# Feed-forward down passes: one tile operation a step, four split buffers for the last pass, and a last tile finished in halves

## The chip, the cores and the metric

One core of one Trainium2 chip runs the kernel as a single program. The metric is the device time of one execution in microseconds (us); the times given are medians of repeated executions. Five engines work side by side, each on its own instruction stream, and meet only at semaphores: TensorE (PE; its weight loads are listed as PEld), VectorE (DVE), ScalarE (ACT), GpSimd (POOL) and SyncE (SP), which here issues the transfers.

## The reference, cut to what matters

The program is one layer of a streaming encoder over 2048 prompt rows and 128 sample rows (8 streams of 16). The change lies in its last stage, the feed forward and the final norm, all in float32:

```
h2 = _rmsnorm(x, g_ffn) * (1 + sc2) + sh2
g = h2 @ f_w_gate
u = h2 @ f_w_up
gconv, new_fconv = _causal_dwconv(g, f_conv, f_conv_w, f_conv_b)
x = x + gt2 * ((jax.nn.silu(gconv) * u) @ f_w_down)
...
y_prompt = _rmsnorm(xp, g_final)
y_sample = _rmsnorm(xs, g_final)
```

The model width is 1024 and the inner width is 2816, which is 22 slices of 128.

## The kernel before

The 2176 rows are 17 tiles of 128 rows: tiles 0 to 15 are prompt, tile 16 is the sample. `feed_forward` takes them in three spans: span 0 has tiles 0 to 5, span 1 has tiles 6 to 11, span 2 (`LAST`) has tiles 12 to 16. For each span all gate and up products come first and leave `mid` (22 slices f, up to 768 columns) in SBUF. Then come two **down passes** a = 0 and a = 1, written (span, a) below: pass (0,0) has tiles 0 to 2, pass (0,1) tiles 3 to 5, and so on; pass (2,0) has tiles 12 to 14 and pass (2,1), the last, only tiles 15 and 16.

A down pass has 22 steps, one for each slice f. Every float32 operand is split into a high and a low part, and three products (high by high, high by low, low by high) are added up in PSUM. So a step needs, in this order: a 512 KB load of the slice of `f_w_down` into `raw[j]` (SP, j = f % 2); its high part `w_hi[j]` and that of `mid`, `m_hi[j]` (ACT); the low parts `w_lo[j]` and `m_lo[j]` (DVE); and 6 matmuls of 512 columns for each tile (PE), 18 a step, or 12 in the last pass. There are two buffers of each kind. ACT may write `w_hi[j]` for step f only when PE has finished step f - 2 (`s_used`), and SP may load `raw[j]` again only when `w_lo[j]` has been made from it (`s_lo`). In pass (2,1) the raw slices alternate between `raw` and two further places, `raw_far`, in columns of `mid` that span 2 does not use. The first and last steps of a pass are written out (`static_until`), the ones between are a hardware loop; pass (2,1) is written out whole.

The tiles of a finished pass are completed inside the first steps of the next pass, or of the next span's gate and up steps. A tile takes five **tile operations**: `gated` (DVE: PSUM sum times the gate, into `prod`), `residual` (DVE: add to the row tile `xr`), `squares` (ACT: sum of squares), two small operations on POOL that make `rstd`, and `finish` (DVE: times `rstd` and the final weight, into the one tile `y`). Then SP issues `store` (512 KB of `y`) and behind it the load of the `xr` of two tiles later. `tile_part(k, ...)` sets which of these follow step k. SP runs its list strictly in order, so a `store` that waits for `y` holds every load that stands behind it.

In passes (0,1), (1,1) and (2,1) the tile operations of the pass before stand like this: two `gated` after step 0, one `residual` after step 1, then `residual`, `gated` and `finish` after step 2, `residual` and `finish` after step 3, `finish` after step 4; the three stores stand in SP's list after the loads of steps 3, 4 and 5. After step 21 of pass (2,1) nothing is left to cover tiles 15 and 16: both are completed one after the other with the engines otherwise empty. In pass (2,1) PE also turns the convolution's kept rows with 22 small matmuls (`turn_tail`, L2987): 16 after step 5 and 6 after step 19.

Of the kernel before, what the change touches and what calls it, by code (L numbers as in the profile page):

```python
# [11 lines left out]
P = 128  # L12
# [2679 lines left out]
def feed_forward_tiles(nc, ctx):  # L2692
# [29 lines left out]
    for name in ("ss", "mean", "rstd"):  # L2722
        tile(name, [P, 2])
    flat = F["mid"][:].rearrange("p f t -> p (f t)")
# [30 lines left out]
def feed_forward(nc, sem, A, O, S, c, F, ffn_first, m_stored):  # L2755
# [4 lines left out]
    with ExitStack() as ctx:  # L2760
# [16 lines left out]
        raw_far = [mid[:, 4 + KD * j:4 + KD * (j + 1), last_width:last_width + P] for j in range(2)]  # L2777
        acc = ps("acc_ps", [P, 4, 2, 512])
# [8 lines left out]
        s_far = [sem(f"w_far_loaded{j}") for j in range(2)]  # L2787
        s_mhi, s_mlo = sem("mid_hi_done"), sem("mid_lo_done")
# [40 lines left out]
        def static_until(s, a):  # L2829

            if pieces(s, a):
                return 1, 1 + KD
            return 3, KF // 2 - 1

        def raw_of(f):

            return raw[f % 2][:].rearrange("p (k c) -> p k c", k=KD) if f % 4 < 2 else raw_far[f % 2]
# [4 lines left out]
        def _(sp):  # L2842
# [12 lines left out]
            def load_dn_last(f):  # L2855
                j, base = f % 2, down_unit(LAST, 1, 0)
                sp.wait_ge(s_lo[j], base + max(0, f // 2 - 1))
                if f % 4 < 2:
# [21 lines left out]
            for s in range(NSP):  # L2880
# [14 lines left out]
                for a in range(NPASS):  # L2895
                    if s == LAST and a == 1:
                        for f in range(KF):
                            load_dn_last(f)
                            if f >= 3 and f - 3 < len(before(s, a)):
                                store(before(s, a)[f - 3])  # L2900
                        continue
                    lo, hi = static_until(s, a)
                    for f in range(2 * lo):
                        load_dn(s, a, f // 2, f % 2)
                        if f >= 3 and f - 3 < len(before(s, a)):
                            store(before(s, a)[f - 3])
# [7 lines left out]
            for i in tiles_of(LAST, 1):  # L2914
                store(i)
            sp.wait_ge(s_tk, 6)
            sp.dma_start(O["s_ffn_conv"][0].rearrange("b j n -> (b j) n"), rows_out[0:16]).then_inc(s_tout, 16)
            sp.dma_start(O["p_ffn_conv"][0, 0], rows_out[16:18]).then_inc(s_tout, 16)
            sp.wait_ge(s_tout, 32)
            sp.wait_ge(s_store, 16 * (NT + 1))  # L2920

        @block.tensor
        def _(pe):
# [32 lines left out]
            def down_step(s, a, q, j):  # L2956
# [3 lines left out]
                for n, i in enumerate(tiles_of(s, a)):  # L2960
# [15 lines left out]
                    for lhs, rhs, begin in ((m_hi, w_hi, start), (m_hi, w_lo, False), (m_lo, w_hi, False)):  # L2976
                        for half in range(2):
                            last = t.matmul(acc[:, pair, half, :], lhs[j][:, cols], rhs[j][:, half * 512:(half + 1) * 512],  # L2978
                                            start=begin, stop=(stop and lhs is m_lo))
                last.then_inc(s_used[j], 1)  # L2980

# [15 lines left out]
            for s in range(NSP):  # L2997
# [5 lines left out]
                for a in range(NPASS):  # L3003
                    lo, hi = static_until(s, a)
                    for f in range(2 * lo):
                        down_step(s, a, f // 2, f % 2)
                    if s == LAST and a == 1:
                        for r in range(4):
                            turn_tail(r, (s_read, first_tile[s] + 3))
                        for f in range(2 * lo, 2 * hi):  # L3010
                            down_step(s, a, f // 2, f % 2)
                        for r in range(4, 6):
                            turn_tail(r, (s_tk, r - 3))
                        for f in range(2 * hi, KF):
                            down_step(s, a, f // 2, f % 2)
                        continue
# [7 lines left out]
        def _(act):  # L3024
# [41 lines left out]
            def down_step_last(f):  # L3066
                j, base = f % 2, down_unit(LAST, 1, 0)
                if f % 4 < 2:
# [3 lines left out]
                act.wait_ge(s_used[j], base + f // 2)  # L3072
                width = len(tiles_of(LAST, 1)) * P
                a_.activation(w_hi[j][:].rearrange("p (k c) -> p k c", k=KD), raw_of(f), ACT.Copy).then_inc(s_hi[j], 1)  # L3074
                a_.activation(m_hi[j][:, 0:width], mid[:, f, HALF:HALF + width], ACT.Copy).then_inc(s_mhi, 1)
# [5 lines left out]
            def tile_part(k, tiles):  # L3081

                if 1 <= k <= len(tiles):
                    squares(tiles[k - 1])

# [5 lines left out]
            for s in range(NSP):  # L3091
# [9 lines left out]
                for a in range(NPASS):  # L3101
                    if s == LAST and a == 1:
                        for f in range(KF):
                            down_step_last(f)
                            tile_part(f, before(s, a))
                        continue
                    lo, hi = static_until(s, a)
                    for f in range(2 * lo):
# [3 lines left out]
                        tile_part(f, before(s, a))  # L3112
# [312 lines left out]
```

## Time and profile before

| | us |
|---|---|
| median of 3 runs | 3045.41 (3045.27 to 3048.97) |
| the profiled execution's own time | 3046.51 |
| span of its profile, first to last instruction | 3044.8 |
| granted TensorE clock, mean over the span | 0.964 of full |
| two down passes of span 0, span 1, span 2 | 191.4, 190.7, 179.4 |
| from the last matmul to the end | 16.0 |

The profile is that of one execution, and its span leaves out 1.7 us at the launch and the end. Sums in this text are made against its own time, 3046.51. A wait is read on the engine that waits: a long idle time of an engine that is not the bound costs nothing.

### The profile page before, as it was taken

What the parts mean: (1) busy time and instruction counts of PE and PEld (TensorE: products, weight loads), DVE (VectorE), ACT (ScalarE), POOL (GpSimd) and SP (SyncE); (2) the same over time, 40 slices, a digit from 0 to 9 for tenths busy, and PEclk for the clock granted to TensorE, in tenths of its full rate; (3) what the DMA queues carried; (4) which work ended last, traced back from release to release, by engine and by line L of the source; (5) the groups of instructions that cost most, each with busy time, mean ns of one, the idle gap of its engine ahead of it and who ended that gap; (6) DMA issues with size and microseconds to landing.
All of it is one profiled execution on the core that took longest, in us unless ns stands there. A gap on an engine that the chain in (4) does not pass through costs nothing.

```text
span 3044.8 us, 42088 instructions
## 1 busy us (share of the span) xinstructions
PE 2824.6 (93%) x16270; PEld 2507.9 (82%) x16270; DVE 1336.9 (44%) x2601; ACT 982.2 (32%) x1698; POOL 253.4 (8%) x413
## 2 busy tenths in 40 slices
PE   4499999999767999997999999999999989999987
PEld 1288888999755777776999997799999879999965
DVE  2333333423245666664333345453344445444444
ACT  1133334423332454453222234322222433222333
POOL 0000000000024334330000000000000000000000
PEclk7699999999878999998999999999999999999998
DMA  9522224222446444334322234432222543322344
GB/s 328 203 75 97 89 90 154 74 88 72 108 169 225 134 136 144 123 112 125 102 64 62 62 110 147 151 104 75 62 62 73 161 150 115 97 74 76 104 147 125
DMA packets 324285, 355.37 MB, mean 117 GB/s; under 512 B 26470, under 2 KB 265674, under 8 KB 323702
## 3 DMA queue, kind: packets, MB, share of 16 engines
q1 hardware_dynamic: 313700, 348.52, 36.1%
q10 hardware_dynamic: 10452, 5.04, 0.7%
q8 instruction: 88, 1.44, 0.2%
q14 instruction: 45, 0.37, 0.0%
HBM read 285.63 MB, written 70.10 MB: 117 GB/s over the span
## 4 chain that ended last, share of the span: by engine, by line
PE 49%; DVE 2%; DMA 1%; issue 1%; ACT 0%; SPq 0%; POOL 0%; DVEq 0%; ACTq 0%
PE acc_ps L2978 14%; PE acc_ps L2934 11%; PE acc_ps L2936 11%; PE acc_ps L2935 11%; DMA f_raw<-in_f_w_down 1%; DMA f_xr<-scratch_x 0%; DVE f_y L3227 0%; DVE f_w_lo L3201 0%; DMA out_y_prompt<-f_y 0%; DVE f_xr L3221 0%; ACT f_w_hi L3074 0%; DVE f_prod L3215 0%; DVE f_h_lo L3253 0%; DVE f_w_lo L3144 0%; DVE f_mid_lo L3205 0%
## 5 line engine op out<-in xcount | busy, mean ns | idle before, releaser
L2934 PE MATMUL acc_ps<-f_h_hi,f_w_hi 128*128 128x384 f32 (+1 forms) x2112 | 689.0, 326 | 2.9 <-DVE f_w_lo L3144 2.8
L2935 PE MATMUL acc_ps<-f_h_lo,f_w_hi 128*128 128x384 f32 (+1 forms) x2112 | 688.7, 326 | 0.0
L2936 PE MATMUL acc_ps<-f_h_hi,f_w_lo 128*128 128x384 f32 (+1 forms) x2112 | 688.6, 326 | 0.0
L3144 DVE TENSOR_TENSOR f_w_lo<-f_raw,f_w_hi 128x1024 fp32r<-128x1024 f32 x242 | 296.4, 1225 | 658.8 <-ACT f_w_hi L3032 656.5
L3032 ACT ACTIVATE f_w_hi<-f_raw 128x1024 fp32r<-128x1024 f32 x242 | 256.5, 1060 | 797.1 <-PE acc_ps L2936 533.3
L2934 PEld LDWEIGHTS acc_ps<-f_h_hi,f_w_hi 128*128 128x128 f32 x2112 | 397.1, 188 | 3.6 <-DVE f_w_lo L3144 3.0
L2935 PEld LDWEIGHTS acc_ps<-f_h_lo,f_w_hi 128*128 128x128 f32 x2112 | 397.2, 188 | 0.1
L2936 PEld LDWEIGHTS acc_ps<-f_h_hi,f_w_lo 128*128 128x128 f32 x2112 | 397.2, 188 | 0.0
L2978 PE MATMUL acc_ps<-f_w_hi,f_mid_hi 128*128 128x512 f32 x748 | 237.8, 400 | 32.0 <-DVE f_mid_lo L3194 16.2
L2978 PE MATMUL acc_ps<-f_w_lo,f_mid_hi 128*128 128x512 f32 x748 | 234.2, 395 | 0.0
L2978 PE MATMUL acc_ps<-f_w_hi,f_mid_lo 128*128 128x512 f32 x748 | 233.7, 394 | 0.0
L881 PE MATMUL p_unit<-w_in_hi,p_ht_hi 128*128 128x512 f32 (+1 forms) x544 | 203.7, 374 | 2.1 <-ACT p_m L487 2.1
L881 PE MATMUL p_unit<-w_in_hi,p_ht_lo 128*128 128x512 f32 (+1 forms) x544 | 200.9, 369 | 0.0
L881 PE MATMUL p_unit<-w_in_lo,p_ht_hi 128*128 128x512 f32 (+1 forms) x544 | 200.5, 369 | 0.0
L2978 PEld LDWEIGHTS acc_ps<-f_w_hi,f_mid_hi 128*128 128x128 f32 x748 | 140.5, 191 | 70.8 <-DVE f_mid_lo L3205 21.2
L940 PE MATMUL p_unit<-p_ht_hi,w_in_hi 128*128 128x384 f32 (+1 forms) x576 | 190.2, 330 | 2.3 <-ACT p_m L474 1.2
L941 PE MATMUL p_unit<-p_ht_lo,w_in_hi 128*128 128x384 f32 (+1 forms) x576 | 189.2, 329 | 0.0
L942 PE MATMUL p_unit<-p_ht_hi,w_in_lo 128*128 128x384 f32 (+1 forms) x576 | 188.6, 327 | 0.0
L2978 PEld LDWEIGHTS acc_ps<-f_w_hi,f_mid_lo 128*128 128x128 f32 x748 | 142.8, 191 | 30.7
L2978 PEld LDWEIGHTS acc_ps<-f_w_lo,f_mid_hi 128*128 128x128 f32 x748 | 142.7, 191 | 30.8
L3130 POOL TENSOR_SCALAR f_mean<-f_ss 128x1 f32<-128x1 f32 x17 | 8.7, 512 | 1606.3 <-ACT f_prod L3079 1606.3
L3179 DVE TENSOR_TENSOR f_mid<-f_gate_on,acc_ps 128x384 f32 (+3 forms) x132 | 64.3, 528 | 162.8 <-PE acc_ps L2936 162.8
(505 smaller groups left out, 4130.2 us busy)
## 6 DMA issues: line engine op xcount, KB each, us to landing
f_raw<-in_f_w_down SPq DMA_DIRECT2D x122, 512.0 KB, 3.4
f_raw<-in_f_w_gate SPq DMA_DIRECT2D x66, 512.0 KB
f_raw<-in_f_w_up SPq DMA_DIRECT2D x66, 512.0 KB, 3.9
w_ada<-in_w_ada SPq DMA_DIRECT2D x12, 2048.0 KB
m_bc<-scratch_bc SPq DMA_DIRECT2D x15, 768.0 KB, 5.0
scratch_tok<-p_m SPq DMA_DIRECT2D x17, 640.0 KB, 3.0
m_tok<-scratch_tok SPq DMA_DIRECT2D x16, 640.0 KB, 4.7
scratch_ht<-p_m SPq DMA_DIRECT2D x17, 512.0 KB, 3.9
```

What stands on the lines that cost most here:

```text
L881: last = t.matmul(dst, a[j][:, k, :], b[:, k, at:at + w], start=(k == 0 and a is th_hi and b is w_hi), stop=(k == KD - 1 and a is th_lo))
L940: t.matmul(dst, w_hi[:, k, cols], hi, start=(k == 0), stop=False)
L941: t.matmul(dst, w_hi[:, k, cols], lo, start=False, stop=False)
L942: last = t.matmul(dst, w_lo[:, k, cols], hi, start=False, stop=(k == KD - 1))
L2934: t.matmul(dst, hi, h2_hi[:, k, cols], start=(k == 0), stop=False)
L2935: t.matmul(dst, hi, h2_lo[:, k, cols], start=False, stop=False)
L2936: last = t.matmul(dst, lo, h2_hi[:, k, cols], start=False, stop=(k == KD - 1))
L2978: last = t.matmul(acc[:, pair, half, :], lhs[j][:, cols], rhs[j][:, half * 512:(half + 1) * 512], start=begin, stop=(stop and lhs is m_lo))
L3032: a_.activation(w_hi[j][:], raw[j][:], ACT.Copy).then_inc(s_hi[j], 1)
L3130: nc.gpsimd.tensor_scalar(mean[:, j:j + 1], ss[:, j:j + 1], 1.0 / D, EPS, ALU.mult, ALU.add).then_inc(s_mean, 1)
L3144: v.tensor_tensor(w_lo[j][:], raw[j][:], w_hi[j][:], ALU.subtract).then_inc(s_lo[j], 1)
L3179: last = v.tensor_tensor(at_f(mid, f)[:, at:at + w], gate_on[:, at:at + w], u_ps[:, b, 0:w], ALU.mult)
```

## The change

Five things change, all in `feed_forward`.

1. Where tile operations of an earlier pass stand in a down pass, there is at most one DVE tile operation after each step (`down_part`), spread over steps 0 to 8 (the two `gated` of step 0 stay together), or in the last pass over steps 2 to 9. The stores move behind the loads of steps 5, 7 and 9, or 6, 8 and 11 in the last pass. `gated` of a pass's first tiles waits for that tile's own last product (`s_down`) and no longer for the whole last step.
2. The last pass has four buffers of each split operand (`wl_hi`, `wl_lo`, `ml_hi`, `ml_lo`), laid in `h2_hi` and `h2_lo`, which nothing reads after the last up product.
3. The splits of its steps 0 and 1 are made inside steps 20 and 21 of pass (2,0), from `raw_far`, loaded early in pass (2,0).
4. Its steps 18 to 21 (`joint_steps`) run first all for tile 15, then all for the first 512 columns of tile 16, then for its other 512. So tile 15 is completed while PE works on tile 16.
5. The last tile is completed in two halves (`last_half`, `finish_halves`), with its mean on DVE, and its result goes out of `prod[1]` in two stores. The small stores of the convolution's rows go out ahead of these.

The diff, cut to its core:

```diff
+        NB4, LW = 4, last_width - HALF
+        h2_flat = [h[:].rearrange("p k t -> p (k t)") for h in (h2_hi, h2_lo)]
+        wl_hi, wl_lo = ([h[:, b * D:(b + 1) * D] for b in range(NB4)] for h in h2_flat)
+        ml_hi, ml_lo = ([h[:, NB4 * D + b * LW:NB4 * D + (b + 1) * LW] for b in range(NB4)] for h in h2_flat)
+        JOINT = KF - NB4
...
-            return 3, KF // 2 - 1
+            return (5 if before(s, a) else 3), KF // 2 - 1
...
             def load_dn_last(f):
-                sp.wait_ge(s_lo[j], base + max(0, f // 2 - 1))
-                if f % 4 < 2:
+                if f >= NB4:
+                    sp.wait_ge(s_llo, f - NB4 + 1)
+                elif f >= 2:
+                    sp.wait_ge(s_lo[j], base)
+                if f % 4 >= 2:
...
                         load_dn(s, a, f // 2, f % 2)
-                        if f >= 3 and f - 3 < len(before(s, a)):
-                            store(before(s, a)[f - 3])
+                        if s == LAST and 1 <= f <= 2:
+                            load_dn_last(f - 1)
+                        for n, at in enumerate((5, 7, 9)):
+                            if f == at and before(s, a):
+                                store(before(s, a)[n])
...
+            def joint_steps():
+                for f in range(JOINT, KF):
+                    pe.wait_ge(s_lmlo, f + 1)
+                    last = last_products(0, f, range(2))
+                last.then_inc(s_down, 1)
+                for half in range(2):
+                    for f in range(JOINT, KF):
+                        last = last_products(1, f, (half,))
+                    last.then_inc(s_half, 1)
...
             def down_step_last(f):
-                act.wait_ge(s_used[j], base + f // 2)
+                if f >= NB4:
+                    act.wait_ge(s_lused, f - NB4 + 1)
...
-                dve.wait_ge(s_used[1], down_unit(s, a, KF // 2 - 1) + 1)
+                if i != tiles_of(s, a)[-1]:
+                    dve.wait_ge(s_down, tiles_done(i))
+                else:
+                    dve.wait_ge(s_used[1], down_unit(s, a, KF // 2 - 1) + 1)
...
+            def last_half(half):
+                cs = slice(half * 512, half * 512 + 512)
+                dve.wait_ge(s_half, half + 1)
...
+                v.tensor_tensor(prod[0][:, cs], acc[:, pair_of[TP + 1], half, :], ffn_gate[:, 1, cs], ALU.mult).then_inc(s_lread, 1)
+                dve.wait_ge(s_lread, half + 1)
+                v.tensor_tensor(xr[0][:, cs], xr[0][:, cs], prod[0][:, cs], ALU.add).then_inc(s_lx3, 1)
...
+                            if 12 <= f < 16:
+                                keep_tail(f - 12)
+                            elif 18 <= f < 20:
+                                keep_tail(f - 14)
...
-            for k in range(4):
-                tile_part(k, tiles_of(LAST, 1))
+            gated(NT - 1)
+            residual(NT - 1)
+            last_half(0)
+            finish(NT - 1)
+            last_half(1)
+            finish_halves()
```

What this does to the order of instructions is shown at three places. Line numbers in rows of the changed kernel are its own. The first place is DVE at the start of pass (0,1): `f_w_lo` and `f_mid_lo` are one step's low parts, `f_prod` is written by `gated`, `f_xr` by `residual`, `f_y` by `finish`. Before:

```order
L3215 TENSOR_TENSOR f_prod<-acc_ps,f_gate 128x1024 x2
L3144 TENSOR_TENSOR f_w_lo<-f_raw,f_w_hi 128x1024
L3194 TENSOR_TENSOR f_mid_lo<-f_mid,f_mid_hi 128x384
L3221 TENSOR_TENSOR f_xr<-f_xr,f_prod 128x1024
L3144 TENSOR_TENSOR f_w_lo<-f_raw,f_w_hi 128x1024
L3194 TENSOR_TENSOR f_mid_lo<-f_mid,f_mid_hi 128x384
L3221 TENSOR_TENSOR f_xr<-f_xr,f_prod 128x1024
L3215 TENSOR_TENSOR f_prod<-acc_ps,f_gate 128x1024
L3227 SCALAR_TENSOR_TENSOR f_y<-f_xr,f_rstd,f_g_fin 128x1024
L3144 TENSOR_TENSOR f_w_lo<-f_raw,f_w_hi 128x1024
L3194 TENSOR_TENSOR f_mid_lo<-f_mid,f_mid_hi 128x384
L3221 TENSOR_TENSOR f_xr<-f_xr,f_prod 128x1024
```

Now, from the same instruction on:

```order
L3282 TENSOR_TENSOR f_prod<-acc_ps,f_gate 128x1024 x2
L3211 TENSOR_TENSOR f_w_lo<-f_raw,f_w_hi 128x1024
L3261 TENSOR_TENSOR f_mid_lo<-f_mid,f_mid_hi 128x384
L3288 TENSOR_TENSOR f_xr<-f_xr,f_prod 128x1024
L3211 TENSOR_TENSOR f_w_lo<-f_raw,f_w_hi 128x1024
L3261 TENSOR_TENSOR f_mid_lo<-f_mid,f_mid_hi 128x384
L3288 TENSOR_TENSOR f_xr<-f_xr,f_prod 128x1024
L3211 TENSOR_TENSOR f_w_lo<-f_raw,f_w_hi 128x1024
L3261 TENSOR_TENSOR f_mid_lo<-f_mid,f_mid_hi 128x384
L3294 SCALAR_TENSOR_TENSOR f_y<-f_xr,f_rstd,f_g_fin 128x1024
L3211 TENSOR_TENSOR f_w_lo<-f_raw,f_w_hi 128x1024
L3261 TENSOR_TENSOR f_mid_lo<-f_mid,f_mid_hi 128x384
```

The third `gated` and the first `finish` no longer stand together with the second `residual`; two and more steps' low parts have come between.

The second place is SP from the first loads of pass (2,1) on. Loads into `f_raw` and `f_mid` (the far places) are slices of the weights, `f_xr<-scratch_x` is the load behind each store. Before:

```order
L2859 DMA f_raw<-in_f_w_down 128x1024 x2
L2861 DMA f_mid<-in_f_w_down 128x8x128 x2
L2876 DMA out_y_prompt<-f_y 128x1024
L2864 DMA f_xr<-scratch_x 128x1024
L2859 DMA f_raw<-in_f_w_down 128x1024
L2876 DMA out_y_prompt<-f_y 128x1024
L2864 DMA f_xr<-scratch_x 128x1024
L2859 DMA f_raw<-in_f_w_down 128x1024
L2876 DMA out_y_prompt<-f_y 128x1024
L2864 DMA f_xr<-scratch_x 128x1024
L2861 DMA f_mid<-in_f_w_down 128x8x128 x2
```

Now:

```order
L2875 DMA f_raw<-in_f_w_down 128x1024 x2
L2877 DMA f_mid<-in_f_w_down 128x8x128 x2
L2875 DMA f_raw<-in_f_w_down 128x1024
L2892 DMA out_y_prompt<-f_y 128x1024
L2880 DMA f_xr<-scratch_x 128x1024
L2875 DMA f_raw<-in_f_w_down 128x1024
L2877 DMA f_mid<-in_f_w_down 128x8x128
L2892 DMA out_y_prompt<-f_y 128x1024
L2880 DMA f_xr<-scratch_x 128x1024
L2877 DMA f_mid<-in_f_w_down 128x8x128
L2875 DMA f_raw<-in_f_w_down 128x1024 x2
L2892 DMA out_y_prompt<-f_y 128x1024
```

The first two rows now load slices 2 and 3 (slices 0 and 1 went out in pass (2,0)), one more slice stands ahead of the first store, and two or three stand between stores where there was one.

The third place is the end of DVE's list. Before:

```order
L3201 TENSOR_TENSOR f_w_lo<-f_raw,f_w_hi 128x1024
L3205 TENSOR_TENSOR f_mid_lo<-f_mid,f_mid_hi 128x256
L3215 TENSOR_TENSOR f_prod<-acc_ps,f_gate 128x1024 x2
L3221 TENSOR_TENSOR f_xr<-f_xr,f_prod 128x1024 x2
L3227 SCALAR_TENSOR_TENSOR f_y<-f_xr,f_rstd,f_g_fin 128x1024 x2
```

Now (the low parts of the last pass are named after the tile `f_h_lo` that holds them):

```order
L3267 TENSOR_TENSOR f_h_lo<-f_mid,f_h_hi 128x1024
L3270 TENSOR_TENSOR f_h_lo<-f_mid,f_h_hi 128x256
L3282 TENSOR_TENSOR f_prod<-acc_ps,f_gate 128x1024
L3288 TENSOR_TENSOR f_xr<-f_xr,f_prod 128x1024
L3334 TENSOR_TENSOR f_prod<-acc_ps,f_gate 128x512
L3336 TENSOR_TENSOR f_xr<-f_xr,f_prod 128x512
L3294 SCALAR_TENSOR_TENSOR f_y<-f_xr,f_rstd,f_g_fin 128x1024
L3334 TENSOR_TENSOR f_prod<-acc_ps,f_gate 128x512
L3336 TENSOR_TENSOR f_xr<-f_xr,f_prod 128x512
L3340 TENSOR_SCALAR f_mean<-f_ss 128x1
L3343 SCALAR_TENSOR_TENSOR f_mean<-f_ss,f_mean 128x1
L3347 SCALAR_TENSOR_TENSOR f_prod<-f_xr,f_rstd,f_g_fin 128x512 x2
```

Of tile 16 only the second half's operations, the mean and the two halves of the result now stand behind the last product; `finish` of tile 15 stands ahead of them.

## Rows read from the trace of the kernel before

**Rows 1.** The page: busy time of each engine, and the chain that ended last by engine.
```profile
PE 2824.6 (93%) x16270; PEld 2507.9 (82%) x16270; DVE 1336.9 (44%) x2601; ACT 982.2 (32%) x1698; POOL 253.4 (8%) x413
...
PE 49%; DVE 2%; DMA 1%; issue 1%; ACT 0%; SPq 0%; POOL 0%; DVEq 0%; ACTq 0%
```
**Rows 2.** Stretches: passes (0,0), (0,1), (1,1), (2,0), (2,1), end; busy, clock, DMA.
```profile
1791.40:1881.30 89.90, 89.90 (x399) 74.42 (x398) 45.21 (x54) 38.29 (x52) 0.00 (x0) 1.00 0.50 159
1881.30:1982.80 101.50, 93.12 (x397) 74.94 (x396) 47.16 (x52) 34.98 (x49) 3.99 (x6) 0.98 0.44 144
...
2438.80:2539.60 100.80, 93.02 (x397) 74.93 (x396) 47.16 (x52) 35.10 (x49) 3.98 (x6) 0.98 0.44 145
...
2849.40:2939.20 89.80, 89.80 (x399) 74.34 (x398) 38.00 (x46) 32.39 (x45) 0.00 (x0) 1.00 0.41 131
2939.20:3028.80 89.60, 73.78 (x287) 54.95 (x285) 46.35 (x57) 31.78 (x48) 3.98 (x6) 0.90 0.45 144
3028.80:3044.80 16.00, 0.00 (x0) 0.00 (x0) 7.19 (x6) 2.29 (x4) 2.33 (x4) 0.59 0.27 78
```
**Rows 3.** PE's waits from 1780 us on: us in total, times, longest.
```profile
PE acc_ps L2978 <- DVE f_mid_lo L3194: 16.2, 10, 4.6
PE acc_ps L2978 <- DVE f_mid_lo L3205: 15.5, 7, 4.4
```
**Rows 4.** Timeline of ACT and DVE: one undisturbed split (start, length, idle before).
```profile
1877.44 1.06 ACT L3032 ACTIVATE f_w_hi<-f_raw 128x1024 fp32r<-128x1024 f32 x1 [2.61 <-PE acc_ps L2978]
...
1878.53 1.23 DVE L3144 TENSOR_TENSOR f_w_lo<-f_raw,f_w_hi 128x1024 fp32r<-128x1024 f32 x1 [2.39 <-ACT f_w_hi L3032]
1879.68 0.55 DVE L3194 TENSOR_TENSOR f_mid_lo<-f_mid,f_mid_hi 128x384 fp32r<-128x384 f32 x1
```
**Rows 5.** Timeline of pass (0,1): DVE's wait for an xr load, PE's longest wait, a pair after.
```profile
1899.40 1.23 DVE L3221 TENSOR_TENSOR f_xr<-f_xr,f_prod 128x1024 f32<-128x1024 f32 x1 [3.92 <-DMA f_xr<-scratch_x]
...
1904.54 0.73 PE L2978 MATMUL acc_ps<-f_w_hi,f_mid_hi 128*128 128x512 f32 x2 [4.61 <-DVE f_mid_lo L3194]
...
1905.82 1.06 PE L2978 MATMUL acc_ps<-f_w_hi,f_mid_lo 128*128 128x512 f32 x2
```
**Rows 6.** Pass (0,1): SP's first store, the load behind it, and the stretch that follows.
```profile
1893.90 0.34 SPq L2876 DMA_DIRECT2D out_y_prompt<-f_y  x1
...
1894.77 0.80 SPq L2852 DMA_DIRECT2D f_raw<-in_f_w_down  x1
...
1895.00:1897.00 2.00, 1.47 (x6) 1.24 (x7) 0.48 (x2) 0.00 (x0) 0.41 (x1) 1.00 1.03 332
```
**Rows 7.** The chain that ended last, middle of pass (2,1): one link from step to step.
```profile
2992.45 1.07 ACT f_w_hi L3074
...
2995.16 3.04 PE acc_ps L2978 x12
```
**Rows 8.** Timeline of PE: the small transposing matmuls in pass (2,1).
```profile
2971.43 1.91 PE L2987 MATMUL acc_ps<-ident,f_tail 128*18 128x128 f32 x16
...
3018.31 0.82 PE L2987 MATMUL acc_ps<-ident,f_tail 128*18 128x128 f32 x6
```
**Rows 9.** Timeline of the end: the pair of gated operations, the last small store.
```profile
3028.81 2.35 DVE L3215 TENSOR_TENSOR f_prod<-acc_ps,f_gate 128x1024 f32<-128x1024 f32 x2 [5.92 <-PE acc_ps L2978]
...
3040.62 0.71 SPq L2918 DMA_DIRECT2D out_p_ffn_conv<-f_mid  x1
```
**Rows 10.** The chain that ended last, at the end: the store of y.
```profile
3035.73 2.62 DMA out_y_prompt<-f_y
```
**Rows 11.** Timeline of POOL: the same operation at the end and in pass (2,1).
```profile
3033.84 0.54 POOL L3133 TENSOR_TENSOR f_rstd<-f_mean,minus_half 128x1 f32<-128x1 f32 x1
...
2951.66 1.40 POOL L3133 TENSOR_TENSOR f_rstd<-f_mean,minus_half 128x1 f32<-128x1 f32 x1
```
**Rows 12.** DVE's groups by form in span 2's gate and up steps.
```profile
L3162 DVE SCALAR_TENSOR_TENSOR f_conv<-f_g_buf,f_tap,f_conv 128x512 f32<-128x512 f32 x22 | 16.5, 752 | 0.8
...
L3149 DVE COPY f_tap<-f_taps 128x4 f32 x16 | 2.6, 162 | 0.0
```

More of the change, by code:

```diff
@@ L2721, in feed_forward_tiles @@
     tile("tap", [P, 4])
-    for name in ("ss", "mean", "rstd"):
+    for name in ("mean", "rstd"):
         tile(name, [P, 2])
+    tile("ss", [P, 4])
     flat = F["mid"][:].rearrange("p f t -> p (f t)")
@@ L2787, in feed_forward @@
         s_far = [sem(f"w_far_loaded{j}") for j in range(2)]
+        s_lhi, s_llo, s_lmhi, s_lmlo, s_lused = (sem("last_" + n) for n in ("w_hi", "w_lo", "mid_hi", "mid_lo", "used"))
+        s_down, s_half, s_lread, s_lx3, s_lss, s_lmean, s_ly = (sem("last_" + n) for n in (
+            "down_tiles", "down_halves", "half_read", "x3", "squares", "mean", "y"))
         s_mhi, s_mlo = sem("mid_hi_done"), sem("mid_lo_done")
@@ L3084, in tile_part, with down_part @@
                     squares(tiles[k - 1])
+            def down_part(k, tiles, at):
+                if tiles and k in at:
+                    squares(tiles[at.index(k)])
             for k in range(KD):
@@ L3120, in _ @@
                     for f in range(2 * hi, KF):
+                        if s == LAST:
+                            down_step_last(f - 2 * hi)
                         down_step(s, a, f // 2, f % 2)
[L3122 to L3123 removed]
+            squares(NT - 1)
+            for half in range(2):
+                cs = slice(half * 512, half * 512 + 512)
+                act.wait_ge(s_lx3, half + 1)
+                a_.activation(prod[0][:, cs], xr[0][:, cs], ACT.Square, accum_out=ss[:, 2 + half:3 + half]).then_inc(s_lss, 1)
         @block.gpsimd
         def _(pool):
[L3127 removed]
+            for i in range(NT):
                 j = i % 2
@@ L3134, in _ @@
                                         ).then_inc(s_rstd, 1)
+            pool.wait_ge(s_lmean, 2)
+            nc.gpsimd.tensor_tensor(rstd[:, 0:1], mean[:, 0:1], c["minus_half"][:, 0:1], ALU.pow).then_inc(s_rstd, 1)
         @block.vector
@@ L3290, in _ @@
                             multiply(s, KF - 1)
-                        tile_part(f, before(s, a))
+                        if f == 0:
+                            for i in before(s, a)[:2]:
+                                gated(i)
+                        down_part(f, before(s, a), 0)
                     with dve.Fori(lo, hi) as q:
```

137 lines of the change are left out of this document (92 added, 45 removed).

## The prediction

> **What bounds the kernel now.** I read the page first, for the bound: PE is busy 93% of the span, and the chain that ended last runs mostly over PE, with DVE at 2% and everything else at 1% or less [rows 1]. So time is won only where PE stands still, runs at a lower clock, or has finished. The table of stretches says where that is [rows 2]. Pass (0,0), which has no tile operations in it, takes 89.9 us with PE busy all of it at full clock; 396 matmuls in 89.9 us are 0.227 us each, and a step of 18 takes 4.09 us. Pass (2,0) agrees (89.8). Passes (0,1) and (1,1) do the same 396 matmuls but take 101.5 and 100.8. Pass (2,1) has 264 matmuls, worth 59.9 us, and takes 89.6 with a mean clock of 0.90. Behind the last product stand 16.0 us without a matmul. The list of waits gives the engine: in all of this stage PE waits only for the last split of a step, DVE's `m_lo`, 16.2 us by L3194 and 15.5 us by L3205 [rows 3].
>
> Then the timeline, for the reason. An undisturbed split starts at 1877.44, just behind the end of the step that frees its buffer, makes its `w_lo` by 1879.76 and its `m_lo` by 1880.23 [rows 4]; the step that needs it starts at the pass boundary, 1881.3 [rows 2]. The split takes 2.8 us of a 4.09 us step and has 1.1 us to spare. One DVE tile operation of 1.2 us behind it still fits ahead of the next split; three do not. In pass (0,1) DVE, with the split of step 4 still to make, waits 3.9 us for an `xr` load, and PE, which needs that split, waits 4.61 us; its next pairs of matmuls take 1.06 us [rows 5], where 512 columns at 2.4 GHz are 0.21 each: the clock has fallen to its level of 1.2 GHz. That `xr` load was issued only behind the store at 1893.90 [rows 6]. In the last pass even an undisturbed step loses: its split takes 2.71 us (2992.45 to 2995.16), and with two buffers it starts only when the step before last is done, so two steps take 2.71 + 3.04 us and the hand-over, about 5.8 [rows 7], where 24 matmuls are 5.44.
>
> **Part 1, one tile operation a step.** DVE has 1.23 + 0.55 + 1.2 = 3.0 us of work in a step of 4.09. After step 0 two `gated` stand together, but they now start when their own tile is done, one and two thirds into the last step of the pass before, so both end about 1.4 us into step 0, before the next `w_hi` is there. If all stalls go, the passes fall to 89.9: 11.6 and 10.9 us. One is left, on SP. The load of step 10 stands behind the store of the third tile, which now waits for a `finish` behind step 8's split. Counted from the pass's start, step 8 starts at 32.7 and its split ends 1.1 earlier; with `finish` the store goes out at 32.9. The load follows 0.9 us later, as there [rows 6]; I take 1.15, as a loop starts there. The earlier trio (store, `xr` load, weight load, 1.57 MB) ran the DMA engines at share 1.03 and 332 GB/s [rows 6], and its `xr` was there at 1899.40 [rows 5], so I take the weight load as landed 4.6 us behind its issue at 1894.77. Here that is 38.7, where `w_hi` could have started at 37.1. Less the 1.1 to spare, PE waits 0.5 us, once in each pass. The bounds are 0 and 1.4 (landing as late as the trio's 5.5 us). The loads of steps 6 and 8 stand behind stores that go out well ahead of their own splits, and cost nothing. Net: 11.6 + 10.9 - 1.0 = 21.5 us.
>
> **Part 2, the last pass.** With four buffers and two splits made ahead, PE is to run 22 steps of 2.72 and the transposes, 1.91 and 0.82 us [rows 8]: 59.9 + 2.7 = 62.6, so 27.0 us less. What hides the splits: steps 0 and 1 are split within steps of 4.09 us in pass (2,0), where DVE then has 1.8 + 1.6 = 3.4 and ACT less, as ACT was busy 32.4 of 89.8 against DVE's 38.0 [rows 2]. In the last pass the split of step 2 ends some 1.5 us in and is wanted at 5.4: a lead of 3.9. From there a step with a tile operation costs DVE 1.6 + 1.25 = 2.85, 0.13 over PE's step, eight times: the lead shrinks by 1 us and grows again from step 10 on. Loads behind a store: that of step 7 goes out about 9.1 us in, lands at 13.7, and its split is ready at 16.4, wanted at 19.0; that of step 12 is ready at 32.0, wanted at 34.5. If landing took 2.5 us longer, that cover would be gone and each later microsecond costs one. The change adds a wait on DVE: `keep_tail(4)` waits for PE's six transposes ahead of step 17, and the low parts of steps 19 to 21 queue behind it, with PE waiting for them. PE ends those transposes at 48.9 and step 17 at 51.6. DVE then needs two copies (0.6 each, half of the 1.23 of [rows 4]) and three splits of 1.6, so step 21 is ready at 54.9; PE wants it after three tile-15 pieces of 1.36, at 55.7. It fits by 0.8. Unknown in the sum: matmuls of one half in a row, all into one bank, which no down pass does now; the gate and up steps do just that 24 times in a row, and PE keeps up there, so nothing is charged. The bound is a lost 0.1 us on 24 matmuls, 2.4.
>
> **Part 3, the end.** Now 16.0 us [rows 2]: two tiles' operations in pairs of 2.35 [rows 9], two stores through one `y`, then small stores. The last small store, issued at 3040.62 [rows 9], holds the end for 4.2 us; it moves ahead. Counted from the last product, what is left is half a `gated` and half a `residual`, each 0.69 (on the line between 0.55 for 384 and 1.23 for 1024 columns [rows 4]; the bounds are these two), half the squares (0.7, between half and all of ACT's 1.06), a small mean on DVE (0.16, as a small copy [rows 12]), POOL's power (0.54 [rows 11]), two result halves (0.75 each [rows 12]), a store (2.62 [rows 10], though of half the size), 0.4 to the end, and 0.3 of hand-overs: 7.6. Ahead of it on DVE stands `finish` of tile 15: two operations of 1.2 behind that tile's last product, squares 1.25, POOL 0.75, then itself 1.28 with hand-overs, which ends about 6.0 behind it, while tile 16's last 24 matmuls take 5.45: 0.6 us late. Together 8.2, so 7.8 us less. Bounds: 6.5 to 10.5.
>
> POOL's power takes 0.54 us at the end, but 1.40 in pass (2,1), beside DVE's tile operations [rows 11]. I take 0.54, as DVE has to wait for `rstd` there. In the Trainium skill, GPSIMD Engine Reference, section Specifications, GpSimd's SBUF interfaces are said to be shared with VectorE and to be contended by a DVE instruction with two SBUF inputs. The addition of tile 16's first half is such an instruction, and it is due while tile 15's mean is made: by the rule at its worst both POOL operations grow by 0.86, and the sum would end 1.7 us later.
>
> **The sum.** 21.5 + 27.0 + 7.8 = 56.3 us. The profiled execution took 3046.5, so 2990.2; the median of the runs is 1.1 us below that execution, so 2989.
>
> **Rivals.** *Stores hold the loads.* In the three changed passes nine stores still stand in front of weight loads, and each sets off three transfers at once. If each of the nine cost 1.5 us (a load 2.6 late, less 1.1 to spare), 13.5 us come back: 3002. For it speaks that this held PE before [rows 5, 6]; against it the distances above, of which only two are over.
>
> *The last pass becomes bound by its transfers.* Its 20 loads, three stores and three `xr` loads are 13.6 MB, 218 GB/s over 62.6 us. At the 159 GB/s that is the highest mean of a pass [rows 2], it would take 86 us, and the time 3012. Against it stand 332 GB/s at full share [rows 6], and the share of 0.50 that goes with 159.
>
> *The clock, and a slower kernel.* The three passes have 1056 matmuls. If PE's clock fell to its lower level in them, each would cost 512 columns at 1.2 GHz, 0.2 us more. From 280 of them on (56.3 / 0.2) the gain is gone; all would give 3200. For it speaks the low clock behind a wait of 4.6 us [rows 5] and 0.90 in pass (2,1); against it that (0,0) and (2,0), of the same steps without such waits, hold 1.00 from end to end [rows 2].
>
> *Nothing moves*, if new waits (`keep_tail`, the ring of four, SP) take about what they free; that needs 50 us of waits that the leads above don't show.
>
> **Chances.** Forecast, 2984 to 2997: 0.72. Loads held: 0.12. Transfers: 0.08. Within 0.2% (6 us, about what a measurement of this kernel can tell from no change): 0.03. Slower: 0.05, most of it the clock. The low end takes all lower bounds (no load late, an end of 6.5) and some room, 2984; the high end takes the held loads in, 3005.
>
> **What would show it.** PE's waits from the first down pass on fall from 31.7 us to about 1, what is left being at step 10 of passes (0,1) and (1,1) and released by a load; those passes take about 90.4 us, pass (2,1) 62.6 at clock 1.00, and from the last product to the end it is 8.2. A PE wait ended by a weight load at other steps, a clock under 1.00 in the last pass, or DVE's `finish` of tile 15 holding the last half by 2 us would each show a step wrong; a wait in the gate and up steps that isn't there now would be a gain given back.

## The result, and the profile after

The changed kernel takes 2995.1 us (median of 4 runs, 2993.8 to 2998.6); the kernel before, run beside it on the same chip, takes 3047.1 (median of 4, 3045.3 to 3049.0). The ratio is 0.9825, with a 95% interval of 0.9811 to 0.9839: 1.75% faster. The forecast was 2989, and both the narrower forecast of 2984 to 2997 and the range of 2984 to 3005 hold the result.

The profiled execution took 2998.57 us, the longest of the four, and its span is 2996.8. The page has the same engine at the same place, with a little less of it [against rows 1]:

```profile
PE 2813.0 (94%) x16270; PEld 2504.1 (84%) x16270; DVE 1337.0 (45%) x2606; ACT 982.5 (33%) x1700; POOL 253.0 (8%) x412
...
PE 50%; DVE 1%; DMA 1%; issue 0%; ACT 0%; SPq 0%; POOL 0%; DVEq 0%; POOLq 0%; ACTq 0%
```

The two spans differ by 48.0 us, but this mixes two things. The first product of the gate steps, before which the change touches nothing, starts at 1422.83 us before and at 1427.88 after: this execution came 5.05 us late into the part that was changed. From that product to the end it is 1621.9 us before and 1568.95 after, so 53.0 less. The experiments below are compared on this **feed-forward length** too, since the start varied from 1421.6 to 1428.8 us over the eight kernels tried, all alike up to there.

The stretches of the changed kernel, in the order and the columns of [rows 2] (busy time of PE, weight loads, DVE, ACT, POOL; then clock, DMA share, GB/s): passes (0,0), (0,1), (1,0), (1,1), (2,0), (2,1) and the end.

```profile
1796.50:1886.30 89.80, 89.80 (x398) 74.35 (x397) 46.23 (x55) 38.30 (x52) 0.00 (x0) 1.00 0.48 159
1886.30:1978.00 91.70, 90.08 (x398) 74.25 (x396) 46.09 (x52) 35.01 (x49) 4.13 (x6) 1.00 0.48 160
...
2344.10:2433.90 89.80, 89.80 (x397) 74.33 (x397) 45.20 (x55) 37.42 (x52) 0.00 (x0) 1.00 0.46 153
2433.90:2525.80 91.90, 90.13 (x398) 74.27 (x397) 46.08 (x52) 35.00 (x49) 4.12 (x6) 1.00 0.49 160
2835.50:2925.30 89.80, 89.80 (x398) 74.35 (x397) 41.77 (x51) 36.31 (x51) 0.00 (x0) 1.00 0.40 132
2925.30:2989.20 63.90, 62.82 (x287) 51.12 (x285) 45.81 (x59) 29.33 (x46) 5.13 (x8) 1.00 0.60 189
2989.20:2996.80 7.60, 0.02 (x1) 0.00 (x0) 3.67 (x7) 0.72 (x2) 0.55 (x1) 0.70 0.35 138
```

The passes (0,1) and (1,1) have lost most of what they had over (0,0) (9.8 of 11.6 us and 8.9 of 10.9), the last pass is down from 89.6 to 63.9, the end from 16.0 to 7.6, and the clock is 1.00 in every pass. PE's waits in all of this stage were 31.7 us [rows 3]; three are left, 1.6 and 1.8 at step 10 of passes (0,1) and (1,1), and 1.1 at step 12 of the last pass:

```profile
PE acc_ps L3001 <- DVE f_mid_lo L3261: 3.4, 2, 1.8
PE acc_ps L3012 <- DVE f_h_lo L3270: 1.1, 1, 1.1
```

The timeline (start, length, idle before and its releaser) of SP, ACT, DVE and PE shows the one in pass (0,1). The rows are in order of start:

```profile
1917.85 1.28 DVE L3294 SCALAR_TENSOR_TENSOR f_y<-f_xr,f_rstd,f_g_fin 128x1024 f32<-128x1024 f32 x1
1919.15 0.34 SPq L2892 DMA_DIRECT2D out_y_prompt<-f_y  x1
1919.54 0.43 SPq L2880 DMA_DIRECT2D f_xr<-scratch_x  x1
1920.31 1.75 SPq L2865 DMA_DIRECT2D f_raw<-in_f_w_down  x2
...
1926.06 1.06 ACT L3087 ACTIVATE f_w_hi<-f_raw 128x1024 fp32r<-128x1024 f32 x1 [5.37 <-DMA f_raw<-in_f_w_down]
...
1927.16 1.23 DVE L3211 TENSOR_TENSOR f_w_lo<-f_raw,f_w_hi 128x1024 fp32r<-128x1024 f32 x1 [5.15 <-ACT f_w_hi L3087]
...
1928.90 0.73 PE L3001 MATMUL acc_ps<-f_w_hi,f_mid_hi 128*128 128x512 f32 x2 [1.62 <-DVE f_mid_lo L3261]
```

The list names DVE's `m_lo` as the releaser, as it did before. Followed upwards it is DVE for ACT, ACT for a load, and that load stood on SP behind the third store, which stood behind `finish`. DVE is the last link of this chain, not its cause.

### The profile page after: what moved, and what is told of

Same layout as the page of the kernel before. It is cut to its first block, busy times and chain, and to the rows that moved or that the text cites. A ratio compares the mean times of both kernels' runs of the same rounds, so it can differ in the third digit from the quotient of the medians.

```text
span 2996.8 us, 41998 instructions
## 1 busy us (share of the span) xinstructions
PE 2813.0 (94%) x16270; PEld 2504.1 (84%) x16270; DVE 1337.0 (45%) x2606; ACT 982.5 (33%) x1700; POOL 253.0 (8%) x412
## 4 chain that ended last, share of the span: by engine, by line
PE 50%; DVE 1%; DMA 1%; issue 0%; ACT 0%; SPq 0%; POOL 0%; DVEq 0%; POOLq 0%; ACTq 0%
PE acc_ps L3001 14%; PE acc_ps L2957 12%; PE acc_ps L2959 12%; PE acc_ps L2958 12%; PE acc_ps L3012 1%; DMA f_mid<-in_f_w_down 0%; DMA f_raw<-in_f_w_down 0%; DVE f_h_lo L3267 0%; DVE f_y L3294 0%; DVE f_h_lo L3361 0%; DVE f_xr L3288 0%; DVE f_h_lo L3270 0%; PE acc_ps L3049 0%; DVE f_prod L3282 0%; ACT f_w_hi L3087 0%
## 5 line engine op out<-in xcount | busy, mean ns | idle before, releaser
L3001 PE MATMUL acc_ps<-f_w_hi,f_mid_hi 128*128 128x512 f32 x660 | 203.6, 389 | 3.4 <-DVE f_mid_lo L3261 3.4
L3001 PE MATMUL acc_ps<-f_w_hi,f_mid_lo 128*128 128x512 f32 x660 | 203.3, 389 | 0.0
L3001 PE MATMUL acc_ps<-f_w_lo,f_mid_hi 128*128 128x512 f32 x660 | 203.1, 389 | 0.0
L3001 PEld LDWEIGHTS acc_ps<-f_w_hi,f_mid_hi 128*128 128x128 f32 x660 | 123.6, 188 | 29.8 <-DVE f_mid_lo L3261 4.2
L3001 PEld LDWEIGHTS acc_ps<-f_w_lo,f_mid_hi 128*128 128x128 f32 x660 | 123.9, 188 | 25.8
L3001 PEld LDWEIGHTS acc_ps<-f_w_hi,f_mid_lo 128*128 128x128 f32 x660 | 123.9, 188 | 25.7
```

## The experiments

Each kernel is the changed one with one edit. Ratios are to the kernel before in the same job: 3045.3 us (median of 9) for the first four, 3048.4 (median of 7) for the last four. The theory under test is that each part pays by its own mechanism (distance between tile operations, a longer ring of splits, the order of the last steps), and that what is left of PE's waits is SP's list.

**1. Passes (0,1) and (1,1) put back to their old schedule.**

```diff
-            return (5 if before(s, a) else 3), KF // 2 - 1
+            return 3, KF // 2 - 1
...
-                        for n, at in enumerate((5, 7, 9)):
-                            if f == at and before(s, a):
-                                store(before(s, a)[n])
+                        if f >= 3 and f - 3 < len(before(s, a)):
+                            store(before(s, a)[f - 3])
...
-                        down_part(f, before(s, a), (2, 3, 7))
+                        tile_part(f, before(s, a))
...
-                        if f == 0:
-                            for i in before(s, a)[:2]:
-                                gated(i)
-                        down_part(f, before(s, a), 0)
+                        tile_part(f, before(s, a))
```

> The changed kernel, with passes (0,1) and (1,1) put back as they were: tile operations packed into steps 0 to 4, stores behind the loads of steps 3, 4 and 5. Theory (the three parts add up, each gives what its stretch lost): the two passes go back from 91.7 and 91.9 us to about 101.5 and 100.8, the last pass (63.9) and the end (7.6) stay, and the time rises by about 18.7 us over the changed kernel, to about 2.6 to 2.9 ms... in numbers 2994.5 + 18.7 = 3013. Rival (the earlier release of each tile's sums, which stays in this kernel, did the work, not the spreading): the two passes stay near 92 and the time within 3 us of the changed kernel.

The 3013 of this text is its sum; the kernel took 3012.2 us, ratio 0.9894 (0.9874 to 0.9914), feed-forward length 1582.8. Its two passes:

```profile
1881.90:1981.30 99.40, 92.46 (x398) 75.04 (x397) 46.21 (x52) 35.10 (x49) 3.98 (x6) 0.98 0.45 148
2437.20:2536.40 99.20, 92.69 (x398) 75.12 (x397) 46.19 (x52) 35.10 (x49) 3.97 (x6) 0.98 0.45 148
```

and PE's waits in all of the stage:

```profile
PE acc_ps L3000 <- DVE f_mid_lo L3260: 13.4, 8, 4.5
```

The waits come back at steps 3 to 6, the longest 4.5 us, and with them the clock of 0.98. So the spreading is worth 99.4 - 91.7 = 7.7 and 99.2 - 91.9 = 7.3 us. Against before (101.5, 100.8) 2.1 and 1.6 us are missing; of the change only the earlier `gated` (the wait on `s_down`) is left in these two passes, so it is the likely cause, though no version tests it by itself.

**2. A ring of two in the last pass, by ACT's wait.**

```diff
-                if f >= NB4:
-                    act.wait_ge(s_lused, f - NB4 + 1)
+                if f >= 2:
+                    act.wait_ge(s_lused, f - 1 if f < JOINT else f - NB4 + 1)
```

> The changed kernel, with ACT made to wait in steps 2 to 17 of the last pass until the step two before is done, as two buffers would make it; order, loads and end stay. Theory (the lead of four buffers hides the splits, the tile operations and late loads): each of some 16 steps costs at least 2.9 instead of 2.72 (3 us), and with no lead each step with a DVE tile operation of 1.25 and each load behind a store adds its own delay, about 8 to 14 us in all; the last pass goes from 63.9 to 72 to 78, the total up 8 to 14. Rival (the spreading alone is enough and the ring is not needed): the last pass rises by 3 us or less.

3000.3 us, ratio 0.9847 (0.9831 to 0.9863), length 1576.0. The last pass takes 71.8 us, 7.9 more:

```profile
2920.20:2992.00 71.80, 66.70 (x287) 51.58 (x285) 46.44 (x59) 32.08 (x50) 5.05 (x8) 0.98 0.54 168
```

That is just under the 72 to 78 of the theory, and the feed-forward length is up by 7.1 where 8 to 14 was expected of the total; the rival, for which the pass rises by 3 us or less, is out.

**3. The last four steps one by one for both tiles**, so that both are done only with step 21.

```diff
-                last.then_inc(s_down, 1)
-                for half in range(2):
-                    for f in range(JOINT, KF):
-                        last = last_products(1, f, (half,))
-                    last.then_inc(s_half, 1)
+                    if f == KF - 1:
+                        last.then_inc(s_down, 1)
+                    last = last_products(1, f, range(2))
+                last.then_inc(s_half, 2)
```

> The changed kernel, with steps 18 to 21 of the last pass one by one for both tiles, so that tile 15's sums are ready 1.4 us before the last product and both halves of tile 16 with it; the halves, the two last stores and the moved small stores stay. Theory (tile 15's operations, about 5 us of DVE, come back onto the path when PE's work no longer covers them): the end grows from 7.6 to about 11.7 us, the total by about 4. Rival (the end is set by the halves and the small stores moved ahead, not by the joint order): within 1 us of the changed kernel.

3000.2 us, ratio 0.9847 (0.9831 to 0.9863), length 1572.2. The last pass and the end:

```profile
2925.80:2989.50 63.70, 62.82 (x287) 51.13 (x286) 42.71 (x56) 27.47 (x42) 4.15 (x6) 1.00 0.61 191
2989.50:3001.00 11.50, 0.02 (x1) 0.00 (x0) 6.68 (x10) 2.60 (x6) 1.27 (x3) 0.71 0.23 91
```

The pass is as long as before the edit, the end 3.9 us longer: that much the order of the last four steps is worth.

**4. The third store one load later in (0,1) and (1,1), two later in the last pass.**

```diff
-            return (5 if before(s, a) else 3), KF // 2 - 1
+            return (6 if before(s, a) else 3), KF // 2 - 1
...
-                            for n, at in enumerate((6, 8, 11)):
+                            for n, at in enumerate((6, 8, 13)):
...
-                        for n, at in enumerate((5, 7, 9)):
+                        for n, at in enumerate((5, 7, 10)):
```

> The changed kernel, with the third store of passes (0,1) and (1,1) behind the load of step 10 instead of step 9 (12 written-out steps instead of 10), and that of the last pass behind the load of step 13 instead of 11. Theory (what is left of PE's waits, 1.8 and 1.9 us at step 10 and 1.2 us at step 12, is a weight load held behind a store that waits for y): all three go, the passes take 89.9, 89.9 and 62.7, and the time falls by about 5 us, to about 2990. Rival (three transfers at once are slow whatever the order): the waits move to the next load behind the store, and the time stays within 2 us.

2989.6 us (median of 5), ratio 0.9814 (0.9799 to 0.9828). PE has no wait left from the first down pass to its last product. Passes (0,1), (1,1), (2,1) and the end:

```profile
1882.80:1972.60 89.80, 89.80 (x398) 74.33 (x397) 46.18 (x52) 35.11 (x49) 4.13 (x6) 1.00 0.50 163
2428.50:2518.30 89.80, 89.80 (x398) 74.36 (x397) 46.15 (x52) 35.12 (x49) 4.12 (x6) 1.00 0.50 164
2917.80:2980.30 62.50, 62.50 (x287) 51.21 (x285) 46.08 (x59) 29.60 (x46) 5.13 (x8) 1.00 0.62 193
2980.30:2987.90 7.60, 0.00 (x0) 0.00 (x0) 3.65 (x7) 0.72 (x2) 0.54 (x1) 0.83 0.36 138
```

The three waits are gone, and nothing has come in their place. The length is 1563.5 us, 5.4 less than the changed kernel's. The ratios to before, 0.9814 and 0.9825, have intervals that overlap, so it is the lengths and the waits, not the medians, that show this version ahead of the changed kernel.

**5. The tile operations of the last pass dense again**, with the ring of four kept.

```diff
-                            for n, at in enumerate((6, 8, 11)):
+                            for n, at in enumerate((5, 6, 7)):
...
-                            down_part(f, before(s, a), (3, 4, 8))
+                            tile_part(f - 1, before(s, a))
...
-                            down_part(f, before(s, a), 1)
+                            tile_part(f - 1, before(s, a))
```

> The changed kernel, with the tile operations of the last pass packed as before into the steps after the first (steps 2 to 5, stores behind the loads of steps 5 to 7), the ring of four and the splits made ahead kept. Theory (the ring's lead of some 4 us covers DVE's bursts, but not DVE's wait for the xr load of tile 14, which is issued behind the first store, and the weight loads held behind the stores): PE waits come back around steps 5 to 8, 3 to 8 us in all; the last pass 66 to 71, against 63.9. Rival 1 (the ring alone covers everything): 62.5 to 64. Rival 2 (the spreading is the main part): 75 or more.

3004.2 us, ratio 0.9857 (0.9838 to 0.9876), length 1580.5. The last pass takes 75.8 us. My theory, that a ring of four covers most of a dense schedule, fell; the second rival was right. The stretch of the pass:

```profile
2918.80:2994.50 75.70, 66.92 (x287) 53.50 (x285) 46.72 (x59) 30.59 (x48) 4.94 (x8) 0.93 0.51 160
```

and the timeline of DVE, ACT and PE around the longest wait:

```profile
2934.03 1.23 DVE L3288 TENSOR_TENSOR f_xr<-f_xr,f_prod 128x1024 f32<-128x1024 f32 x1 [3.94 <-DMA f_xr<-scratch_x]
...
2935.29 1.06 ACT L3134 ACTIVATE f_prod<-f_xr 128x1024 f32<-128x1024 f32 x1 [6.55 <-DVE f_xr L3288]
...
2936.35 1.04 ACT L3129 ACTIVATE f_h_hi<-f_mid 128x1024 fp32r<-128x1024 f32 x1
...
2939.04 1.22 PE L3012 MATMUL acc_ps<-f_h_hi 128*128 128x512 f32 x2 [5.86 <-DVE f_h_lo L3270]
2940.05 1.05 PE L3012 MATMUL acc_ps<-f_h_lo,f_h_hi 128*128 128x512 f32 x2
```

DVE's `residual` waits 3.9 us for an `xr` load; ACT's `squares` waits for that `residual`, 6.6 us, and the next split's high parts stand behind it in ACT's list. So one late `xr` stops both engines that make splits, even with four buffers. PE then stands for 5.9 us, and its pairs of matmuls go at 1.05 us, the lower clock; PE's busy time is 66.9 us where version 4 needs 62.5, so some 4.4 of the 13.3 us between them are work at the lower clock, the rest waits. Not all of these are the late `xr`: the second longest, 2.6 us, ends on the weight load behind the third store, which ACT could start on only 7.6 us after its issue (2941.72 to 2949.33).

**6. The first two splits later**: steps 0 and 1 of the last pass are split behind those of steps 20 and 21 of pass (2,0), no longer between them.

```diff
-                        if s == LAST:
-                            down_step_last(f - 2 * hi)
+                    if s == LAST:
+                        down_step_last(0)
+                        down_step_last(1)
```

> The changed kernel, with the splits of the last pass's steps 0 and 1 made behind those of steps 20 and 21 of pass (2,0), and no longer between them. Theory (with four buffers of their own these splits wait for nothing that PE does, and DVE has them done some 2 us ahead of the pass boundary): no change, the last pass within 0.5 us and the time within 2 us of the changed kernel. Rival (the place inside steps 20 and 21 is what takes the wait off the start of the pass): PE waits 1 to 3 us at steps 0 to 2.

2997.2 us, ratio 0.9828 (0.9808 to 0.9848), length 1568.7, against 1568.95. PE doesn't wait at steps 0 to 2. Its only wait in the pass is that at step 12, here 1.95 us by the distance between its matmuls; over the kernels that leave the last pass from step 2 on as it is, this one was between none and 1.95. Where the first two splits stand is worth nothing that shows. They are still made ahead, though: DVE ends the second one at 2922.09, and the last pass starts at 2924.26:

```profile
2921.67 0.42 DVE L3271 TENSOR_TENSOR f_h_lo<-f_mid,f_h_hi 128x256 fp32r<-128x256 f32 x1
```

What making them ahead is worth, against making them inside the last pass, no version tests.

**7. Held, but without the transfers around it**: in passes (0,1) and (1,1) SP waits for the third `y` ahead of the load of step 10, as in the changed kernel, but issues that load first and the store and the `xr` load behind it.

```diff
-            return (5 if before(s, a) else 3), KF // 2 - 1
+            return (6 if before(s, a) else 3), KF // 2 - 1
...
-                        for n, at in enumerate((5, 7, 9)):
+                        for n, at in enumerate((5, 7, 10)):
...
+                        if f == 9 and before(s, a):
+                            sp.wait_ge(s_y, before(s, a)[2] + 1)
```

> The changed kernel, with SP in passes (0,1) and (1,1) still waiting for the third tile's y ahead of the load of step 10, but the store and the xr load themselves issued behind that load (12 written-out steps). The load of step 10 is as late in its issue as before, with no other transfer in front of it. Theory (the wait comes from both together: an issue 2 us late and a landing of 5.8 instead of 3.4 us behind store and xr load): no PE wait at step 10, the two passes 89.8, the time 3.5 us below the changed kernel. Rival (the late issue alone is enough): a wait of 1 us or more stays at step 10.

2989.9 us, ratio 0.9804 (0.9785 to 0.9824), length 1564.5. Both passes take 89.8 us and have no wait. SP around the load of step 10, and ACT's split of it:

```profile
1916.46 0.33 SPq L2865 DMA_DIRECT2D f_raw<-in_f_w_down  x1
1916.83 0.43 SPq L2892 DMA_DIRECT2D out_y_prompt<-f_y  x1
...
1920.63 1.06 ACT L3089 ACTIVATE f_w_hi<-f_raw 128x1024 fp32r<-128x1024 f32 x1 [2.63 <-DMA f_raw<-in_f_w_down]
```

The load, held until the third `y` is there, goes out at 1916.46 and ACT can start on it 4.2 us later, where the changed kernel's needed 5.75. In version 4 the load of step 10 is not held, and the next one, which stands behind the store, has time enough: ACT doesn't wait for it. So the hold alone costs PE nothing, and a load behind a store that isn't late costs nothing either; the wait at step 10 needs both, the late issue and the store ahead of the load. The expectation has one thing wrong: the load is not as late in its issue as before. It leaves 32.8 us into the pass where the changed kernel's leaves 34.0, because the store and the `xr` load are no longer issued first. So of the 2.8 us by which ACT starts earlier, 1.2 are the time in which SP issues the two, and 1.6 the shorter landing; the landing alone was not tried.

**8. The small stores of the convolution's rows back behind the last stores.**

```diff
-            sp.wait_ge(s_tk, 6)
-            sp.dma_start(O["s_ffn_conv"][0].rearrange("b j n -> (b j) n"), rows_out[0:16]).then_inc(s_tout, 16)
-            sp.dma_start(O["p_ffn_conv"][0, 0], rows_out[16:18]).then_inc(s_tout, 16)
             store(NT - 1)
...
+            sp.wait_ge(s_tk, 6)
+            sp.dma_start(O["s_ffn_conv"][0].rearrange("b j n -> (b j) n"), rows_out[0:16]).then_inc(s_tout, 16)
+            sp.dma_start(O["p_ffn_conv"][0, 0], rows_out[16:18]).then_inc(s_tout, 16)
```

> The changed kernel, with the two small stores of the convolution's rows put back behind the last store of y. Theory (they hold the end as they did before, by 4.2 us from their last issue): the end grows from 7.6 to about 9.8 us, the total by about 2. Rival (they land beside the last stores, unseen): the end stays at 7.6.

2995.1 us, ratio 0.9827 (0.9807 to 0.9847), length 1570.1. The end takes 9.55 us, 1.9 more than the changed kernel's 7.61, as expected. The total can't show it: the feed forward started at 1422.3 us here and at 1427.9 in the changed kernel's profile.

## Why the prediction was right, and where its sizes were off

| term | predicted | measured | tested by |
|---|---|---|---|
| one tile operation a step, (0,1) and (1,1) | 21.5 | 9.8 + 8.9 = 18.7 | 1, 4, 7 |
| the last pass | 27.0 | 25.7 | 2, 4, 5, 6 |
| the end | 7.8 | 8.4 | 3, 8 |
| sum | 56.3 | 52.8 | |

The measured column is the difference of the two tables of stretches. The length of the feed forward gives 53.0; the rest of it, the gate and up steps and the other passes, moved by 0.2. The forecast in us was 6.1 too low: 3.5 are the sum. Of the other 2.6, 1.7 are the base: the kernel before, run beside the changed one, took 3047.1 where the forecast starts from a median of 3045.4. All 2.6 are less than the spread of the part ahead of the feed forward.

**The step that was mis-sized is the landing of a load behind a store**, taken as 4.6 us. Part 1 had the place right, and the times of the issues: counted from the start of pass (0,1), the store of the third tile was forecast at 32.9 and went out at 32.85, its weight load 1.15 us behind it and 1.16. But ACT could start on the load only 5.75 us after its issue, longer than the upper bound of 5.5 too. PE waited 1.8 us by the distance between its matmuls (1.6 in the list) where 0.5 was taken and 1.4 was the bound. This was not one bad execution: in the six kernels that keep this schedule (the changed one and versions 2, 3, 5, 6 and 8) the twelve such loads took 5.1 to 5.9 us, and PE's waits were 1.0 to 1.8 in the list. What was taken as a bound lies in the middle.

The 4.6 was read off the wrong transfer. It is the time from the weight load's issue to the arrival of the `xr` load, which stands ahead of it. The weight load's own landing was in the trace of the kernel before: behind the second and the third store of pass (0,1), ACT started on the slice 5.8 and 7.2 us after its issue, having waited for it:

```profile
1902.71 0.79 SPq L2852 DMA_DIRECT2D f_raw<-in_f_w_down  x1
...
1907.40 17.35 SPq L2852 DMA_DIRECT2D f_raw<-in_f_w_down  x5
...
1908.54 1.06 ACT L3032 ACTIVATE f_w_hi<-f_raw 128x1024 fp32r<-128x1024 f32 x1 [5.38 <-DMA f_raw<-in_f_w_down]
...
1914.59 1.06 ACT L3032 ACTIVATE f_w_hi<-f_raw 128x1024 fp32r<-128x1024 f32 x1 [4.58 <-DMA f_raw<-in_f_w_down]
```

The same size was wrong in the last pass. Step 12's split was forecast to be ready at 32.0 us for a PE that wants it at 34.5. The text set the point where this cover is gone: a landing 2.5 us longer. It took 7.1 us, just 2.5 longer (issue, store ahead of it, `finish`, and ACT's start on the slice):

```profile
2948.99 1.28 DVE L3294 SCALAR_TENSOR_TENSOR f_y<-f_xr,f_rstd,f_g_fin 128x1024 f32<-128x1024 f32 x1
...
2950.30 0.34 SPq L2892 DMA_DIRECT2D out_y_prompt<-f_y  x1
2950.69 0.43 SPq L2880 DMA_DIRECT2D f_xr<-scratch_x  x1
2951.16 1.80 SPq L2877 DMA_DIRECT2D f_mid<-in_f_w_down  x2
...
2958.29 1.06 ACT L3129 ACTIVATE f_h_hi<-f_mid 128x1024 fp32r<-128x1024 f32 x1 [7.97 <-DMA f_mid<-in_f_w_down]
```

The load also left 1.2 us later than forecast, 25.9 us into the pass where 24.7 was meant (32.0 less 4.6 for the landing and 2.7 for the split): the `finish` ahead of its store stood on DVE behind the split of step 9, whose slice, loaded behind a store too, had taken 7.0 us. The longer landing used up the cover, and the 1.2 us are the wait of 1.1 that PE has. Version 4, where the store no longer stands ahead of that slice, takes 62.50 us, against the forecast 62.6: the rest of this term was right. By the prediction's own sign, a PE wait ended by a weight load at another step than 10, this step was wrong. So the rival of held loads, given a chance of 0.12, was right in its mechanism, at three places of nine, with about 5 us in all and not 13.5.

**The other steps held.** The clock is 1.00 in all passes, so the cost at the lower clock fell away with most of the waits; versions 1, 2 and 5 bring both back together (0.98, 0.98 and 0.93). The last pass has a DMA share of 0.60 at 189 GB/s and, in version 4, 0.62 at 193 with PE busy throughout: it isn't bound by transfers. Matmuls of one half in a row into one bank cost nothing, as 62.50 us leave no room for a charge. `keep_tail` holds nothing up: PE has no wait behind step 12.

**How the parts of the last pass add up.** Without the ring of four it is 7.9 us longer, without the spreading 11.9, with the first splits moved about the same; all together are 25.7. The other 6 us were not taken apart: they come when ring and spreading are gone together, or they belong to the splits made ahead, which no version gave up. The prediction had one mechanism for the whole, splits that start too late; version 5 shows a second inside it, the late `xr` that stops ACT as well as DVE.

**The end** came out 0.6 us shorter than forecast. The chain at the end, piece by piece:

```profile
2983.82 1.24 DVE f_prod L3282
...
2985.07 1.24 DVE f_xr L3288
...
2986.33 1.16 ACT f_prod L3134 x2
...
2987.57 0.44 POOL f_mean L3195
...
2988.09 0.54 POOL f_rstd L3198
2988.63 3.63 issue
...
2992.88 0.75 DVE f_prod L3347
```

It runs through tile 15, as the 0.6 us for `finish` of that tile said: PE's last product ends at 2989.2, `finish` (2988.66 to 2989.94 on DVE) comes out of the way 0.7 later. The last store, of half the size, needed 2.1 us from its issue at 2994.32 where 2.62 was taken for a whole one; that is most of the difference.

**POOL beside DVE.** By the rows, 0.54 was taken for the power, and that is what it took, with DVE idle beside it. The mean ahead of it took 0.44 us while DVE added the first half of tile 16. At the end of the kernel before, the same operation took 0.19 with DVE idle and 1.05 beside a `finish` (the first row is the changed kernel's, the others are of the kernel before):

```profile
2987.26 0.69 DVE L3336 TENSOR_TENSOR f_xr<-f_xr,f_prod 128x512 f32<-128x512 f32 x1
...
3033.57 0.19 POOL L3130 TENSOR_SCALAR f_mean<-f_ss 128x1 f32<-128x1 f32 x1 [73.18 <-ACT f_prod L3079]
...
3034.70 1.05 POOL L3130 TENSOR_SCALAR f_mean<-f_ss 128x1 f32<-128x1 f32 x1 [0.32 <-ACT f_prod L3079]
```

So the contention that the Trainium skill tells of (GPSIMD Engine Reference, Specifications) agrees with this trace in kind. It cost 0.25 us here; the worst case of the prediction, 1.7 us, did not happen, as only the mean met DVE's addition.

**What stays open.** What moves the start of the feed forward by up to 7 us between executions of the same code was not tried, nor why the wait at step 12 varies from none to 1.95 us.

## What to carry to other kernels

A load that stands in an in-order list behind a store waits twice, for the result that the store carries and then for the transfers issued with it; give such a load either an issue ahead of the store or a whole step more of distance, and price its landing in that company, not alone. When a wait list names a compute engine, follow it upwards before acting: here DVE was named each time, and a line of SP's list was the cure, worth 5 us for three numbers. Four buffers did not cover a late operand that stops the very engines which fill them, so spread the operations that can be late first, and lengthen the ring second.

## What of the hardware was not expected

- A 512 KB load of the weights lands 3.4 us behind its issue by the median of 120 in the profile of the changed kernel, but ACT could start on it 4.2 us after an issue with store and `xr` load behind it, and 5.1 to 5.9 with both ahead of it in passes (0,1) and (1,1). In the last pass, where more loads follow at once, it was 7.0 and 7.1 with both ahead of it, for slices that land in `mid` as eight pieces of 128 columns. The pieces are not shown to be the cause: in version 4 a slice that lands whole in `raw` took 6.8 behind a store and an `xr` load too (2926.63 to 2933.46).
- The same code up to the feed forward took 1421.6 to 1428.8 us in the profiles of nine kernels. On totals alone a difference of 2 us, as that of version 8, can't be seen in four runs; the stretch where it lies shows it in one.
